# First attention: squares summed in two rounded halves, with GpSimd's subtractions placed between the cuts of weights

## The reference, cut to what matters

```python
def diff_attention(q, k, v, q_g, k_g, rel_bias, lam, subln_g, lambda_init):
    q = rmsnorm(q, q_g)      # over each 64 columns: q * rsqrt(mean(q*q) + eps) * g
    k = rmsnorm(k, k_g)
    def one_block(args):     # 128 query positions
        logits = jnp.einsum('bqhcd,bkhcd->bhcqk', q_blk, k).astype(jnp.float32) * scale
        logits = logits + bias[None, :, None]
        logits = jnp.where(rel >= 0, logits, -jnp.inf)
        p = jax.nn.softmax(logits, axis=-1)
        attn = p[:, :, 0] - lam * p[:, :, 1]
        return jnp.einsum('bhqk,bkhe->bqhe', attn.astype(v.dtype), v)
    ...
    out = rmsnorm(out, subln_g) * (1.0 - lambda_init)
```

## Time and profile before

| | |
|---|---|
| median of three runs | 1899.05 us (1898.58 to 1899.74) |
| the profiled execution | 1899.73 us |
| its span, from the first to the last instruction in the profile | 1897.9 us |
| granted clock of PE | 0.999 |
| PE busy | 1879.9 us, 99% of the span |
| POOL busy | 1402.7 us, 74% |
| DVE busy | 924.4 us, 49% |
| ACT busy | 552.4 us, 29% |
| shares of the chain of waits that ended last | PE 93%, DVE 4%, ACT 1%, DMA 1% |

### The profile page before, as it was taken

One profiled execution on the slowest core, in us unless ns is written; L12 is line 12 of the kernel. 1 busy time (PEld: TensorE's weight loads), 2 busy tenths in 40 slices (PEclk: granted clock), 3 DMA queues, 4 the chain that ended last, 5 costly groups with the idle time before them and its releaser, 6 DMA issues.

```text
span 1897.9 us, 23852 instructions
## 1 busy us (share of the span) xinstructions
PE 1879.9 (99%) x8791; PEld 1554.5 (82%) x8791; DVE 924.4 (49%) x1494; ACT 552.4 (29%) x1109; POOL 1402.7 (74%) x1676
## 2 busy tenths in 40 slices
PE   9999999999999999999999999999999999999998
PEld 7777788888888888888888888888899888888886
DVE  5888788753442212135776673334644542122124
ACT  5666544331121101022366551101322211010012
POOL 6554479999887777778666667777898777777773
PEclk9999999999999999999999999999999999999999
DMA  5222123333333333333443323333343333333321
GB/s 172 78 78 70 48 81 95 98 110 113 99 91 100 100 94 95 100 97 95 119 132 92 82 63 100 100 95 112 104 119 104 89 100 91 98 100 99 90 83 61
DMA packets 345941, 182.67 MB, mean 96 GB/s; under 512 B 14989, under 2 KB 341811, under 8 KB 345828
## 3 DMA queue, kind: packets, MB, share of 16 engines
q1 hardware_dynamic: 343890, 177.88, 32.5%
q10 hardware_dynamic: 1938, 3.29, 0.7%
...
## 4 chain that ended last, share of the span: by engine, by line
PE 93%; DVE 4%; ACT 1%; DMA 1%; issue 1%; SPq 0%; DVEq 0%; POOL 0%; POOLq 0%; ACTq 0%
PE bank L724 28%; PE bank L726 27%; PE bank L728 27%; PE bank L860 2%; PE bank L812 1%; PE bank L838 1%; PE bank L1076 1%; PE bank L1078 1%; PE bank L1077 1%; PE bank L792 1%; PE bank L1142 1%; PE bank L823 1%; PE bank L1162 1%; DMA FBIAS_ROWS<-decay_rows 0%; PE bank L906 0%
## 5 line engine op out<-in xcount | busy, mean ns | idle before, releaser
L643 POOL TENSOR_TENSOR WL<-RAW,WH 128x256 fp32r<-128x256 f32 (+2 forms) x1276 | 1029.2, 837 | 29.5 <-POOL WH L637 0.4
L637 POOL TENSOR_SCALAR WH<-RAW 128x1024 fp32r<-128x1024 f32 (+3 forms) x331 | 356.3, 1076 | 405.4 <-PE bank L728 356.9
L724 PE MATMUL bank<-HH,WH 128*128 128x512 f32 x1560 | 618.2, 396 | 0.5 <-DVE HL L1782 0.5
L728 PE MATMUL bank<-HH,WL 128*128 128x512 f32 x1560 | 614.1, 394 | 0.0
L726 PE MATMUL bank<-HL,WH 128*128 128x512 f32 x1560 | 610.7, 391 | 0.0
L724 PEld LDWEIGHTS bank<-HH,WH 128*128 128x128 f32 x1560 | 293.3, 188 | 60.5 <-issue 5.9
L728 PEld LDWEIGHTS bank<-HH,WL 128*128 128x128 f32 x1560 | 293.1, 188 | 59.1 <-issue 1.9
L726 PEld LDWEIGHTS bank<-HL,WH 128*128 128x128 f32 x1560 | 293.3, 188 | 58.0 <-issue 3.1
L2040 DVE TENSOR_TENSOR X<-X,bank 128x512 f32<-128x512 f32 x80 | 55.0, 687 | 234.5 <-PE bank L728 234.5
L724 PE MATMUL bank<-UH,WH 128*128 128x512 f32 x256 | 99.6, 389 | 0.0
L726 PE MATMUL bank<-UL,WH 128*128 128x512 f32 x256 | 99.6, 389 | 0.0
...
## 6 DMA issues: line engine op xcount, KB each, us to landing
RAW<-in_w_in SPq DMA_DIRECT2D x107, 512.0 KB, 3.6
RAW<-in_w_up SPq DMA_DIRECT2D x32, 512.0 KB, 3.8
RAW<-in_w_down SPq DMA_DIRECT2D x32, 512.0 KB, 3.6
RAW<-in_w_ffn_gate SPq DMA_DIRECT2D x22, 512.0 KB, 3.5
RAW<-in_w_ffn_up SPq DMA_DIRECT2D x22, 512.0 KB, 3.6
RAW<-in_w_xkv SPq DMA_DIRECT2D x16, 512.0 KB, 3.8
RAW<-in_w_ffn_down SPq DMA_DIRECT2D x16, 512.0 KB, 3.8
RAW<-in_w_proj_attn SPq DMA_DIRECT2D x8, 512.0 KB, 3.6
```

Source lines behind the costliest of these rows:

```text
L637: nc.gpsimd.tensor_scalar(WH[:, s, 0:k, :], RAW[:, s, 0:k, :], 1.0, 1.0, ALU.mult, ALU.mult).then_inc(S_[f"hi_made{s}"], 1)
L643: nc.gpsimd.tensor_tensor(WL[:, s, own_tiles, :], RAW[:, s, own_tiles, :], WH[:, s, own_tiles, :].bitcast(F32), ALU.subtract).then_inc(S_[ ...
L724: mm(psum[s][:, 0:n], WH[:, s, k, :], hi(k), start=(k == 0), stop=False)
L728: last = mm(psum[s][:, 0:n], WL[:, s, k, :], hi(k), start=False, stop=(k == tiles - 1))
```

## The change

1. A constant HALVESR, `halves` in float32r, is made at the start by a copy on DVE.
2. For heads 1 to 7 ACT writes each square twice, once to SQ and once, rounded, to SQH. POOL subtracts (`squares_lo`, new) into SQL. PE sums SQH and SQL in two float32r matmuls. Head 0 keeps the float32 product.
3. POOL makes the two copies of the keys in the other rows (`keys_copied`, new), which ACT made as the last two steps of `k_hi`.
4. Both of these stand on POOL before the cut of unit ("qkv", h + 1, 1), for h from 1 to 6, and for h = 7 before that of ("first", 0, 1); `decay_scales` stands one cut later than before.
5. On PE the first statistic moves from behind the seven transposes into share[1], after 14 of its 24 products; the second comes after 8 of the 10 products of share[2] instead of 5.
6. DVE takes the queries before the third combination. Their norm follows the take of the keys, the low half of the output (L1964) comes before the probabilities, and the low halves of queries and keys are spread between the four of the probabilities by part. ACT's order follows: the first inverse root comes before the square of the keys.
7. The scores of head h wait for part 0 of queries and keys at the first score and for part 1 at the second.
8. The output's square uses SQH and SQL, side 1, in place of OSH and OSL, and its high half is a second Square instead of a Copy. The numbers that later waits on `pool_made` ask for are shifted by what is added.

In the diff the declarations of the tiles and the shifted numbers of later waits are left out, and so are the unchanged lines.

```diff
+            def squares_lo(h, side):
+                pool.wait_ge(S_["a_qk_sq"], 4 * h + 2 * side)
+                nc.gpsimd.tensor_tensor(M1["SQL"][:, side, :], M1["SQ"][:, side, :],
+                                        M1["SQH"][:, side, :].bitcast(F32), ALU.subtract).then_inc(S_["pool_made"], 1)
+            def keys_copied(h):
+                pool.wait_ge(S_["a_qk_norm"], 2 * h + 2)
+                for part in range(2):
+                    nc.gpsimd.tensor_scalar(M1["KH"][other_rows(part), part, :], M1["QN"][own_rows(part), 1, :],
+                                            1.0, 1.0, ALU.mult, ALU.mult).then_inc(S_["pool_made"], 1)
+                pool.wait_ge(S_["pool_made"], 4 * h + 1)
...
-                if (name, it, j) == ("qkv", 4, 1):
+                n = units.place[name, it, j]
+                if n % 3 == 1 and 2 <= n // 3 <= HEADS:
+                    for side in range(2):
+                        squares_lo(n // 3 - 1, side)
+                    keys_copied(n // 3 - 1)
+                if (name, it, j) == ("qkv", 4, 2):
...
-                pe.wait_ge(S_[tag + "_qk_hi"], 2 * h + 22 if kind is KIND_SWA else 6 * h + 6)
-                pe.wait_ge(S_[tag + "_qk_lo"], 2 * h + 12 if kind is KIND_SWA else 4 * h + 4)
+                parted = kind is KIND1 and h
+                pe.wait_ge(S_[tag + "_qk_hi"], {KIND1: 4 * h + (5 if h else 6), KIND_FOX: 6 * h + 6, KIND_SWA: 2 * h + 22}[kind])
+                pe.wait_ge(S_[tag + "_qk_lo"], 2 * h + 12 if kind is KIND_SWA else 4 * h + (3 if parted else 4))
+                if parted:
+                    pe.wait_ge(S_["pool_made"], 4 * h)
...
+                    if t == 1 and parted:
+                        pe.wait_ge(S_["a_qk_hi"], 4 * h + 6)
+                        pe.wait_ge(S_["a_qk_lo"], 4 * h + 4)
+                        pe.wait_ge(S_["pool_made"], 4 * h + 1)
...
-                run(steps, share[1])
+                if kind is KIND1:
+                    run(steps, share[1][0])
+                    if stats:
+                        stats(0)
+                    run(steps, share[1][1])
+                else:
+                    run(steps, share[1])
...
-                if stats:
-                    stats(0)
...
-                pe.wait_ge(S_["a_qk_sq"], 2 * h + 1 + side)
-                stat("a", n + side, halves[:], M1["SQ"][:, side, :])
+                if h == 0:
+                    pe.wait_ge(S_["a_qk_sq"], 1 + side)
+                    stat("a", n + side, halves[:], M1["SQ"][:, side, :])
+                    return
+                pe.wait_ge(S_["pool_made"], 4 * h - 2 + side)
+                pe.wait_ge(S_["a_stat_free"], n + side)
+                mm(STAT[:], HALVESR[:], M1["SQH"][:, side, :], start=True, stop=False)
+                mm(STAT[:], HALVESR[:], M1["SQL"][:, side, :], start=False, stop=True).then_inc(S_["a_stat"], 1)
...
-                    steps, share = steps0, ((2,) * 8, 18, (4, 4), 3)
+                    steps, share = steps0, ((2,) * 8, (12, 6), (6, 2), 3)
...
-                    share = (2,) * 4 + (3,) * 4, 20, (5, 5), 3
+                    share = (2,) * 4 + (3,) * 4, (20, 0), (5, 5), 3
...
-                    steps, share = chain(*[from_h("qkv", h + 1, j) for j in range(3)]), ((3,) * 5 + (4,) * 3, 24, (5, 5), 2)
+                    steps, share = chain(*[from_h("qkv", h + 1, j) for j in range(3)]), ((3,) * 5 + (4,) * 3, (14, 10), (8, 2), 2)
...
-                mm(STAT[:], onesr[:], M1["OSH"][:], start=True, stop=False)
-                mm(STAT[:], onesr[:], M1["OSL"][:], start=False, stop=True).then_inc(S_["a_stat"], 1)
+                mm(STAT[:], onesr[:], M1["SQH"][:, 1, :], start=True, stop=False)
+                mm(STAT[:], onesr[:], M1["SQL"][:, 1, :], start=False, stop=True).then_inc(S_["a_stat"], 1)
...
-            def q_hi(tag, M):
-                for part in range(2):
+            def q_hi(tag, M, parts=(0, 1)):
+                for part in parts:
...
-            def q_hi1(h):
+                if h:
+                    A(M1["SQH"][:, side, :], M1["QN"][:, side, :], ACT.Square).then_inc(S_["a_qk_sq"], 1)
+            def q_hi1(h, parts=(0, 1)):
...
-                q_hi("a", M1)
+                q_hi("a", M1, parts)
...
+                    rsqrt_stat("a", 3 * h + 2, 1.0 / 64, M1["RQ"][:, 0, :])
...
-                        rsqrt_stat("a", 3 * h + 2, 1.0 / 64, M1["RQ"][:, 0, :])
+                        q_hi1(h + 1, (0,))
...
-                        q_hi1(h + 1)
-                    if n >= 2 and not last:
-                        k_hi1(h + 1, (0,) if n == 2 else (1, 2, 3))
+                        q_hi1(h + 1, (1,))
+                        k_hi1(h + 1, (0,))
+                    if n == 2 and not last:
+                        k_hi1(h + 1, (1,))
...
-                A(M1["SQ"][:, 2, :], M1["OR"][:], ACT.Square).then_inc(S_["a_o_sq"], 1)
-                act.wait_ge(S_["a_o_sq"], 3 * h + 1)
-                A(M1["OSH"][:], M1["SQ"][:, 2, :], ACT.Copy).then_inc(S_["a_o_sq"], 1)
+                A(M1["SQ"][:, 1, :], M1["OR"][:], ACT.Square).then_inc(S_["a_o_sq"], 1)
+                A(M1["SQH"][:, 1, :], M1["OR"][:], ACT.Square).then_inc(S_["a_o_sq"], 1)
...
-            def softmax(tag, M, kind, h, row_max, v_lo, combine, between=None, done="_probs", second=None):
+            def softmax(tag, M, kind, h, row_max, v_lo, combine, between=None, done="_probs", second=None, ahead=None):
...
+                    if ahead and i == NB - 1:
+                        ahead()
...
+            own.wait()
+            own.mark(V.tensor_copy(HALVESR[:], halves[:]))
...
-                    if i == 3 and not last:
-                        take_qk1(h + 1, 0)
...
-                        second=(lambda: out_sq_lo1(h - 1)) if h else None)
+                        second=(lambda: out_sq_lo1(h - 1)) if h else None,
+                        ahead=None if last else lambda: take_qk1(h + 1, 0))
...
+                    norm_qk1(h + 1, 3 * h + 2, 0)
+                if h:
+                    out_lo1(h - 1)
...
-                    if n == 1 and not last:
-                        norm_qk1(h + 1, 3 * h + 2, 0)
-                    if n == 1 and h:
-                        out_lo1(h - 1)
...
+                        q_lo("a", M1, 4 * (h + 1) + 3, (0,))
...
-                        q_lo("a", M1, 6 * (h + 1) + 1)
-                    if n == 3 and not last:
-                        for part in range(2):
-                            k_lo("a", M1, 6 * (h + 1) + 3, part)
+                        q_lo("a", M1, 4 * (h + 1) + 3, (1,))
+                    if n >= 2 and not last:
+                        k_lo("a", M1, 4 * (h + 1) + 5, n - 2)
...
-                V.tensor_tensor(M1["OSL"][:], M1["SQ"][:, 2, :], M1["OSH"][:].bitcast(F32), ALU.subtract
-                                ).then_inc(S_["a_o_sq"], 1)
+                V.tensor_tensor(M1["SQL"][:, 1, :], M1["SQ"][:, 1, :], M1["SQH"][:, 1, :].bitcast(F32),
+                                ALU.subtract).then_inc(S_["a_o_sq"], 1)
```

12 lines of the change are left out of this document (6 added, 6 removed).

## The result

The changed kernel takes 1922.76 us (1922.05 to 1923.22) against 1899.36 of the kernel before (medians of four runs each): 1.0122 times as long, 95% interval 1.0111 to 1.0134, or 23.4 us more. The profiled execution took 1922.37 us with a span of 1920.2. The forecast was 1910.5 with a range to 1919: the direction was right, the size half of it.

A forecast was written before the change was run, and what follows sets the result against it. PE, busy 99% of the span, bounds the kernel. Six heads at +1.2 us (7.2), less 1.2 already paid in heads 1 and 2, plus 5.5 once, gave +11.5 on 1899.05: 1910.5 us, range 1902 to 1919.

The forecast's parts named there:

- PE saved per head: Two statistics per head on PE, each 0.46 us as a pair instead of 0.86: 0.8 us saved per head.
- hand-offs and new order per head: New PE waits per head: 0.4 first statistic, 0.3 second, 0.3 and 0.2 at values(2) and values(3).
- POOL beside DVE per head: POOL's copies and cuts slow DVE by 0.43 us per instruction; two in the k_lo pair count: 0.8, bounds 0 and 1.7.
- an ordinary head: Net cost per head of savings, hand-off waits and POOL beside DVE: +1.2 us, 26.6 instead of 25.4.
- once, head 3: decay_scales on POOL behind the keys' copies delays head 4's first subtraction: PE waits 5.5 us once, bounds 3.5 and 7.5.
- first statistic: Moved up on PE, it waits for POOL's subtraction of the squares, landing at 204.9: 0.4 us, bounds 0 and 0.8.
- second statistic: Waits for keys, two Squares and a subtraction despite its later place; 0.3 us, bounds 0 and 1.2.
- third value product: values(2) at the head's end, behind DVE's fuller queue: 0.3 us more wait, bounds 0 and 0.5.
- fourth value product: values(3) at the head's end, behind DVE's fuller queue: 0.2 us more wait, bounds 0 and 0.5.
- the k_lo pair: Two DVE instructions making the keys' low halves beside POOL, in the chain without slack: 0.43 us each, priced 0.8.
- Heads 0 and 1: Head 0: saving of 0.8 against equal waits, 0. Head 1 already pays 0.50 of POOL beside DVE, taken off.
- The rival built on the rule: DVE's k_lo instructions each wait a whole POOL subtraction, 0.74 not 0.43: +0.7 per head, 1914.7 us; chance 0.16.

The follow-up runs named there:

- e12: Kernel before with two-pass statistics, POOL's subtractions between its cuts, old order of DVE and ACT, and POOL's weight subtractions 8 columns wide in heads 2 to 7: 1897.20 us, 0.9990.
- e6: Changed kernel with decay_scales moved to before the cut of (rnn, 0, 2) and POOL's weight subtractions 8 columns wide in qkv units of heads 2 to 7: 1905.17 us, 1.0032.
- e7: Kernel before with POOL's weight subtractions 8 columns wide in the qkv units of heads 2 to 7: 1895.62 us, 0.9984.
- e1: Changed kernel with decay_scales moved from before the cut of (qkv, 4, 2) to before that of (rnn, 0, 2): 1916.38 us, 1.0086.
- e3: As e1, with the first statistic behind the seven transposes again: 1925.10 us, 1.0134.
- e8: Kernel before with two-pass statistics, POOL subtracting between its cuts, and the next cut held until DVE has made the queries' low halves: 1912.89 us, 1.0076.
- e11: As e6, with the copies of the keys back on ACT: 1901.21 us, 1.0010.

## Why the prediction was wrong

The direction was right and the rise was 11.9 us larger than forecast: 7.4 of it lies in the six ordinary heads' term, 1.8 in head 3, 1.3 in head 1, 0.8 in head 0 and 0.6 outside the heads.

By cause, with the runs that show it:

| term, us | forecast | measured |
|---|---|---|
| PE saved per head | −0.8 | −0.6 at pairs of 0.57; −0.8 by pairs of 0.46 |
| hand-offs and new order per head | +1.2 | +1.7: 0.7 (25.15 − 0.8 to e12's 25.07) and 1.0 (e12 to e6) |
| POOL beside DVE per head | +0.8 | +1.7 (e6), less 0.2 paid before (e7) |
| an ordinary head | +1.2 | +2.43 |
| once, head 3 | +5.5 | +7.3 |
| head 0 | 0 | +0.80 |
| head 1, beyond an ordinary one's | −0.5 | +0.77 |
| head 2, beyond an ordinary one's | −0.7 | −0.72 |

An ordinary head in one line, from the runs: 25.38 − 0.23 (e7) − 0.8 + 0.72 (e12) + 1.0 (e6) + 1.73 (e1) = 27.80. It closes by construction, as each term is the distance to the next run.

By place, without that assumption: for each place in head 6 the distance from the start of the product before it, less the same distance in head 6 of the kernel before. A pair of the new statistic counts 0.57 to the next start, the float32 product 0.86; the fourth value product has 0.07 more in its own first matmul.

| place on PE, us | forecast | measured |
|---|---|---|
| seventh score | 0 | +0.50 (0.85 − 0.35) |
| first statistic | +0.4 | +1.11 (1.34 − 0.23) |
| the two statistics themselves | −0.8 | −0.58 |
| second statistic | +0.3 | +0.22 |
| third value product | +0.3 | +0.21 |
| fourth value product | +0.2 | +0.42 |
| next mark (the k_lo pair) | +0.8 | +0.56 |
| sum | +1.2 | +2.44 |

**The step that failed** is the one that priced POOL beside DVE: "Two of those covered (the k_lo pair) stand in the chain without slack". The pair was priced right (0.43 each forecast; 1.12 + 1.22 − 1.40 = 0.94 measured, in the changed kernel as in e6), and PE felt 0.56 of it. But the chain in the scores has no slack either: the prediction names two combinations beside the train and leaves them out of the sum, and does not name the output's norm. With it fails the term of the first statistic, 0.4 with 0.8 as its upper bound, because it took the last row maximum from the trace of the kernel before, where POOL rested beside it. There four instructions lost 1.6 us (0.38 + 0.48 + 0.40 + 0.36). They made the last row maximum 1.1 us later, which delayed the seventh score by 0.46 and ACT's squares after it, and the subtraction itself took 0.26 more beside DVE, so that the first statistic waited 0.95 and not 0.4. Together these two places cost PE 1.61 us where 0.4 was forecast, which is nearly all that an ordinary head was short of. e6 took the subtractions away from beside DVE and with them both waits, and in head 3 of the changed kernel, without cuts beside the scores, the seventh score does not wait either.

**The hand-offs** were 0.5 short per head by cause, but e12 and e6 are the only evidence for how they split; which part of the new DVE order costs the 1.0 was not tried one by one. e3, e8 and e11 show why single terms mislead: each removed all or most of the wait it aimed at, and a wait came back at a later place.

**The once** was right in its mechanism and in PE's wait: 6.61 − 0.95 = 5.66 against 5.5. The time of the head grew by 7.3 because of a consequence I had not priced, 2.4 us of PE at the lower clock, less 0.6 for the seventh score, which does not wait in that head, and 0.2 at its end. e1 confirms the cause.

**Heads 0 and 1** I had taken as covered. Head 0 waits 1.54 us for its first aSQL. Head 1 waits 1.21 at the seventh score (ordinary heads 0.46). In its trace DVE does three LOGT operations (0.64, 0.20 and 0.42 us) ahead of the first row maximum. They alone do not make the wait: in e6 they stand in the same place (0.29, 0.20 and 0.20), the seventh score of head 1 does not wait, and the head takes 26.51 us. So there too it is POOL's cuts beside DVE; head 0 was not tested by itself.

**The Trainium skill's rule** ("SBUF — State Buffer", section "Terms": the loser of the shared port pair "fully blocks") bears on e1 and e6. The four DVE instructions in the scores of head 6 lost 0.36 to 0.48 us against POOL instructions of 0.7 to 1.5: less than a whole one, and POOL lost too (L637 1.49 instead of 1.05). The most that one lost was 0.69 (a 128x128 combination in head 1, 1.04 instead of 0.35). What blocks whole instructions in turn and what shares would both give such rows; no run here tells them apart. The rival built on the rule (1914.7) was nearer to the time, but by a wrong count of instructions, as the forecast.
